# Recurrent mixer of a two-block network: scan exponentials issued as two steps, readouts one step behind the states, the output's square two steps ahead of its sum

## The reference, cut to what matters

```python
    def step(state, inp):
        qc, kc, gc, vc = inp
        L = jnp.cumsum(gc, axis=2)
        o_inter = jnp.einsum('bhtk,bhkv->bhtv', qc * jnp.exp(L), state)
        ...
        L_end = L[:, :, -1:, :]
        new_state = jnp.exp(L_end[:, :, 0, :])[..., None] * state + jnp.einsum(
            'bhsk,bhsv->bhkv', kc * jnp.exp(L_end - L), vc)
        return new_state, o_inter + o_intra
    ...
    o_fw, _ = hgrn2_chunk_scan(q, k_fw, g_fw, v, s_fw)
    o_bw, _ = hgrn2_chunk_scan(flip(q), flip(k_bw), flip(g_bw), flip(v), s_bw)
    return readout(o_fw + flip(o_bw), gate), y_c
```

## Time and profile before

| what | us |
|---|---|
| median of three runs | 3117.19 (3116.17 to 3118.52) |
| profiled execution | 3118.59 |
| its span | 3116.8 |
| TensorE busy | 2762.1 (89%) |
| VectorE busy | 1563.2 (50%) |
| ScalarE busy | 1029.5 (33%) |
| GpSimd busy | 1050.7 (34%) |
| mixer with dense products beside it, from 2180 to 2661 us | 481 |
| the last head alone, from 2661 to 2709 us | 48 |

### The profile page before, as it was taken

One profiled execution on the slowest core, in us unless ns is written; L12 is line 12 of the kernel. 1 busy time (PEld: TensorE's weight loads), 2 busy tenths in 40 slices (PEclk: granted clock), 3 DMA queues, 4 the chain that ended last, 5 costly groups with the idle time before them and its releaser, 6 DMA issues. The chain is left out here.

```text
span 3116.8 us, 37300 instructions
## 1 busy us (share of the span) xinstructions
PE 2762.1 (89%) x14376; PEld 2272.6 (73%) x14376; DVE 1563.2 (50%) x2423; ACT 1029.5 (33%) x1739; POOL 1050.7 (34%) x510
## 2 busy tenths in 40 slices
PE   1799869989999799999799999997888888699998
PEld 1587548868888577777588888875777777578886
DVE  3433435664454436565755555545556565532223
ACT  2323323232222434343421112124545444332222
POOL 2213343444444411110233223332434343334443
PEclk9899889999999899999899999998999999899999
DMA  5423222433333100000133333311111111022222
GB/s 194 147 88 107 90 83 100 154 122 135 128 129 129 64 18 24 18 23 20 49 127 116 121 115 122 129 62 39 55 41 48 41 48 41 28 81 95 95 95 75
DMA packets 78529, 264.56 MB, mean 85 GB/s; under 512 B 8464, under 2 KB 12688, under 8 KB 78352
## 3 DMA queue, kind: packets, MB, share of 16 engines
q1 hardware_dynamic: 70416, 248.67, 23.0%
q10 hardware_dynamic: 7648, 12.19, 1.2%
q0 software_dynamic: 288, 1.31, 0.1%
HBM read 258.99 MB, written 3.15 MB: 84 GB/s over the span
## 5 line engine op out<-in xcount | busy, mean ns | idle before, releaser
L1908 POOL TENSOR_TENSOR SLO<-RAW,SHI 128x1024 fp32r<-128x1024 f32 (+1 forms) x336 | 812.8, 2420 | 1691.3 <-ACT SHI L1753 1691.3
L1753 ACT ACTIVATE SHI<-RAW 128x1024 fp32r<-128x1024 f32 (+1 forms) x336 | 346.5, 1034 | 1183.9 <-PE PS L2165 1149.7
L2163 PE MATMUL PS<-HLh,SHI 128*128 128x512 f32 x1680 | 691.0, 411 | 21.4 <-DVE HLl L1973 14.3
L2164 PE MATMUL PS<-HLl,SHI 128*128 128x512 f32 x1680 | 662.6, 394 | 0.0
L2165 PE MATMUL PS<-HLh,SLO 128*128 128x512 f32 x1680 | 661.9, 394 | 0.0
L2163 PEld LDWEIGHTS PS<-HLh,SHI 128*128 128x128 f32 x1680 | 320.1, 191 | 115.6 <-issue 38.1
L2165 PEld LDWEIGHTS PS<-HLh,SLO 128*128 128x128 f32 x1680 | 319.7, 190 | 69.7
L2164 PEld LDWEIGHTS PS<-HLl,SHI 128*128 128x128 f32 x1680 | 320.8, 191 | 66.0 <-issue 8.1
L2163 PE MATMUL PS<-hh,SHI 128*128 128x512 f32 (+1 forms) x944 | 352.7, 374 | 11.4 <-DVE hl L2055 9.9
L2164 PE MATMUL PS<-hl,SHI 128*128 128x512 f32 (+1 forms) x944 | 348.4, 369 | 0.0
L2165 PE MATMUL PS<-hh,SLO 128*128 128x512 f32 (+1 forms) x944 | 348.0, 369 | 0.0
(11 more groups left out here) (229 smaller groups left out, 4048.3 us busy)
## 6 DMA issues: line engine op xcount, KB each, us to landing
RAW<-in_k_w SPq DMA_DIRECT2D x316, 512.0 KB, 3.2
ADA<-in_k_w SPq DMA_DIRECT2D x132, 512.0 KB, 4.1
early<-in_k_w SPq DMA_DIRECT2D x12, 512.0 KB, 10.8
RAW<-in_k_w SPq DMA_DIRECT2D x20, 256.0 KB, 2.6
XL<-in_xT ACTq DMA_DIRECT2D x1, 2048.0 KB, 12.0
bi<-in_k_bias ACTq DMA_DIRECT2D x16, 128.0 KB, 2.2
out<-XL SPq DMA_DIRECT2D x8, 256.0 KB, 2.1
bi<-in_k_bias ACTq DMA_DIRECT2D x8, 192.0 KB, 2.5
```

Of the source, the lines that this page charges most:

```text
L1753: eng.activation(u.hi, u.w, ACT.Copy).then_inc(S["a_hi"], 1)
L1908: eng.tensor_tensor(u.lo, u.w, u.hi.bitcast(F32), ALU.subtract).then_inc(S["g_lo"], 1)
L2163: eng.matmul(st.out, lh, rh, start=st.first and j == 0, stop=False)
L2164: eng.matmul(st.out, lh, rl, start=False, stop=False)
```

## The change

Three things change, all in the mixer.

1. `ScanE` becomes `ScanK` (keys) and `ScanQ` (queries). One generator now covers both directions. The keys' exponentials of d=1 are issued right after the transposes of d=0, and their transposes after the third readout of d=0. The queries' exponentials of d=1 are issued after the fourth readout of d=0, which they need because there is one `eq` buffer.
2. In a direction, state step n first makes its own matmul and then reads out the state of step n-1 (for n of 3 and 4, and the two last readouts follow in two further places).
3. `HOutA` loses its square, which becomes the step `HSquare`; two yields stand between the two.

```diff
-    def hscan(h, d, O, first):
+    def hscan(h, O):
...
+        def keys(d):
+            xcell, _, pend, _, t_pd = H[(h, d)]
+            ek = W["ek"].next()
+            t_eke[d] = tick("a_eke", 5 if d == 0 else 1)
+            put(ScanK(d, parts_of(xcell)[1], pend.ap, ek.ap, order[d], [xcell.rdy, t_pd], ek.free, t_eke[d]))
+            return ek
+
+        def queries(d):
...
+            put(ScanQ(d, parts_of(xcell)[0], pend.ap, eq.ap, q.ap, [xcell.rdy, t_pd], eq.free, q.rdy, t_eqe[d], t))
+            return eq, t
+
+        def turned(d, ek):
...
+                put(ScanT(ek.ap, kt.ap, order[d][n0:n1], n0, b.ap, t_eke[d], b.free, t, kt.free, t2))
...
+        def read(d, n, S, eq, t_eq):
...
+            put(ScanO(O.ap[:, 128 * j:128 * j + 128], S.ap, eq.ap[:, 128 * j:128 * j + 128], d == 0 and n == 0,
+                      [S.rdy, t_eq, O.free], t))
...
+        ek = keys(0)
         yield
...
+        eq, t_eq = queries(0)
         yield
...
+        kt, t_kt = turned(0, ek)
+        ek = keys(1)
+        yield
+        for d in range(2):
...
+                put(ScanS(b.ap[:, 0:128], kt.ap[:, 128 * n:128 * n + 128], vv[:, i, :], old.ap if S else None, S2.ap,
+                          dec.ap[:, i:i + 1], [t_kt[n], vc.rdy], b.free, t, [old.rdy if S else None, t_pd, S2.free], t2))
...
+                if n > 2:
+                    read(d, n - 3, S[n - 2], eq, t_eq)
+                yield
...
+            read(d, 2, S[3], eq, t_eq)
+            if d == 0:
+                kt, t_kt = turned(1, ek)
+            yield
+            t = read(d, 3, S[4], eq, t_eq)
+            eq.free = [t]
+            pend.free = [t_pd, t_eke[d], t_eqe[d]]
+            if d == 0:
+                eq, t_eq = queries(1)
+            yield
...
+            t1 = tick("a_osq")
+            put(HSquare(O.ap, f.ap, t, f.free, t1))
+            yield
+            yield
             b = take()
             work[0] += 2048
-            t1, t2, t3, t4 = tick("a_osq"), tick("p_ostat"), tick("a_oln"), tick("a_ors")
-            put(HOutA(O.ap, f.ap, b.ap, r.ap, t, f.free, t1, b.free, t2, r.free, t3, t4))
+            t2, t3, t4 = tick("p_ostat"), tick("a_oln"), tick("a_ors")
+            put(HOutA(f.ap, b.ap, r.ap, t1, b.free, t2, r.free, t3, t4))
```

More of the change, by code:

```diff
@@ L1480, in hscan @@
         vv = vc.ap.rearrange("p (t n) -> p t n", t=6)[:, :, 128 * (h % 2):128 * (h % 2) + 128]
[L1481 to L1488, removed]
@@ L1489, in hscan @@
-        yield
[L1490 to L1499, removed]
-        yield
[L1501 to L1504, removed]
-                work[0] += 512
[L1506 to L1520, removed]
-            yield
@@ L1522, in hscan @@
[L1522 to L1531, removed]
+        order = ([4, 5, 0, 1, 2], [5, 4, 3, 2, 1])
+        lats = ([0, 1, 2, 3], [3, 2, 1, 0])
+        t_eke, t_eqe = {}, {}
+        def keys(d):
[4 more added lines that the diff above has]
+            return ek
@@ new lines, in queries @@
+        def queries(d):
+            xcell, _, pend, _, t_pd = H[(h, d)]
+            eq = W["eq"].next()
+            t_eqe[d], t = tick("a_eqe", 1 if d == 0 else 4), tick("g_eqm")
+            put(ScanQ(d, parts_of(xcell)[0], pend.ap, eq.ap, q.ap, [xcell.rdy, t_pd], eq.free, q.rdy, t_eqe[d], t))
+            return eq, t
+        def turned(d, ek):
+            kt, t_kt = W["kt"].next(), []
+            for n0, n1 in ((0, 2), (2, 5)):
+                b = take()
+                work[0] += 512 * (n1 - n0)
+                t, t2 = tick("p_kt"), tick("a_kt")
+                put(ScanT(ek.ap, kt.ap, order[d][n0:n1], n0, b.ap, t_eke[d], b.free, t, kt.free, t2))
+                give(b, t2)
+                t_kt += [t2] * (n1 - n0)
+            ek.free = [t]
+            return kt, t_kt
@@ new lines, in read @@
+        def read(d, n, S, eq, t_eq):
+            j = lats[d][n]
+            work[0] += 512
+            t = tick("p_so")
+            put(ScanO(O.ap[:, 128 * j:128 * j + 128], S.ap, eq.ap[:, 128 * j:128 * j + 128], d == 0 and n == 0,
+                      [S.rdy, t_eq, O.free], t))
+            S.free.append(t)
+            return t
+        ek = keys(0)
+        yield
+        eq, t_eq = queries(0)
+        yield
+        kt, t_kt = turned(0, ek)
+        ek = keys(1)
+        yield
+        for d in range(2):
+            _, _, pend, dec, t_pd = H[(h, d)]
+            S = []
+            for n, i in enumerate(order[d]):
+                b = take()
+                work[0] += 512
+                S2, old = W["S"].next(), S[-1] if S else None
+                t, t2 = tick("p_sk"), tick("v_state")
+                put(ScanS(b.ap[:, 0:128], kt.ap[:, 128 * n:128 * n + 128], vv[:, i, :], old.ap if S else None, S2.ap,
+                          dec.ap[:, i:i + 1], [t_kt[n], vc.rdy], b.free, t, [old.rdy if S else None, t_pd, S2.free], t2))
+                S2.free, S2.rdy = [], [t2]
+                if S:
+                    old.free.append(t2)
+                give(b, t2)
+                S.append(S2)
+                if n > 2:
+                    read(d, n - 3, S[n - 2], eq, t_eq)
+                yield
+            kt.free = [t]
+            dec.free = [t2]
+            read(d, 2, S[3], eq, t_eq)
+            if d == 0:
+                kt, t_kt = turned(1, ek)
+            yield
+            t = read(d, 3, S[4], eq, t_eq)
[4 more added lines that the diff above has]
+            yield
@@ L1616, in hhead @@
         O = take()
-        sc = chain(hscan(h, 0, O, True), hscan(h, 1, O, False))
+        sc = hscan(h, O)
         alive = True
@@ L1942, in lev_a @@
                     eng.tensor_tensor(r, r, st.q, ALU.mult).then_inc(S["g_lev"], 1)
-            own = {Dma: dma_, Split: split, Square: square_, HRope: hrope, GateX: gate_x, DiagK: diag_k, ScanE: scan_e,
+            own = {Dma: dma_, Split: split, Square: square_, HRope: hrope, GateX: gate_x, DiagK: diag_k, ScanQ: scan_q,
                    LevA: lev_a}
```

39 lines of the change are left out of this document (22 added, 17 removed).

## The result

The changed kernel takes 3045.02 us (median of 4 runs, 3043.29 to 3048.43) against 3117.43 us for the kernel before beside it: a ratio of 0.9769, with a 95% interval of 0.9752 to 0.9786, or 72 us less. The forecast was 3054 us, 9 us too high and inside its range of 3036 to 3092. The profiled execution of the changed kernel took 3048.43 us (span 3046.6), so the two profiled executions are 70.2 us apart. One thing should be stated exactly, since the list of what changes says it otherwise (its second point): a readout now stands one state behind where it stood. It reads the state of step n-1 in the kernel before and the state of step n-2 now, next to the matmul of step n.

What follows compares the result with a forecast made beforehand. In the mixer TensorE has the most work yet idles, waiting in order for small results. Terms -14.4 - 10.6 - 7.5 - 22 - 2 - 13 + 12 - 7 = -64.5 from 3118.6 gave 3054 us, range 3036 to 3092.

Steps and rivals of the forecast that it cites:

- Backward keys: Backward transposes' 17.8 us of waits for the keys' exponentials go, 14.4 of them beside dense work: -14.4 us.
- Square and levels: Sum over the square stops waiting, -10.6 us; first-level product waits -12.3, new diagonal-product waits for key sum +4.8, together -7.5.
- Readouts: Readouts' waits for states outside the last head, 28.5 us, shrink to 6.5: -22 us, bounds 0 to -28.5.
- Forward keys: Of the forward transposes' 9.0 us of waits for the keys' exponentials, 2 us go; bounds 0 and -7.3.
- Clock: TensorE's slow spells behind nine waits of 2.7 us and more go, 1.5 us each: -13 us; bounds 0 and -14.
- What came back: A faster TensorE meets other results earlier, such as level products and `kt` copies: +12 us, between 0 and 23.
- the sign of being wrong that I had named for them: The forecast would be wrong if the copies of `kt` made the state matmuls wait; no size given.
- Last head: Last head alone: readouts off the update chain -3.2, backward keys 3, `HOutB` 1; -7 us, bounds -2 and -12.
- the one in which VectorE and ScalarE take the pace: A head's chain on VectorE and ScalarE sets the pace once the waits go: -34, 3084 us; chance 0.18.

Runs made afterwards that it cites:

- ke: Changed kernel with GpSimd's key sum issued earlier, ahead of the weight subtractions; 0.9736 of the kernel before, 10 us less than the changed kernel.
- f_k: Kernel before with only the keys' and queries' exponentials split and the backward keys issued earlier, readouts and square as before; ratio 0.9957 to it, -13 us.
- l2g: Changed kernel with the second level's product on GpSimd instead of VectorE; 0.9766 of the kernel before, no change against the changed kernel.

## Why the prediction was right, step by step

Taken by stage, the account holds. The profiled executions are 70.2 us apart. Beside dense work TensorE's idle time fell by 49.0 us, for which the terms of waits, with what I gave back, make 44.5; its busy time fell by 17.0 us, for which I had 13 of clock; the last head gave 4.7 where I had 7. Taken by part it holds less well, as follows.

*Backward keys (-14.4).* The waits went as said. The gain is 10 to 15 us by the four pairs of kernels that differ in this part alone (72 - 62, 57 - 46, 30 - 15, 13), and that includes the clock and the last head, for which I had 4.5 and 3 more. So this term was too large by a third or more. With the keys alone readouts wait longer, up to 5.21 us, behind a gate on VectorE; and with the readouts moved most of the keys' waits are gone without it.

*Square and levels (-10.6 and -7.5).* With three spells of clock and 1 us at the end my sum was -24; measured -15 to -17 in all four pairs. The square's 10.6 us and the first levels' 12.3 went: neither shows after, though 10.3 us at other levels do. The key sum's wait was foreseen as 2.4 us twice and is 2.26 and 2.27. Not foreseen was its 5.18 us in the last head, where it was 1.9. With the square alone, copies of `kt` cost 6.4 us, where the kernel before has 2.1.

*Readouts (-22).* This part was too small in the sum. With its clock and last head it made -30; measured are -42 to -47 us in the four pairs. Readouts waited 6.2 us in the end, where I had let 6.5 stay, so the term by itself is right; what the part takes along from the keys (14.4 us of waits beside dense work down to 4.9, by the place that it adds to a direction) and from the clock (11 us of busy time, 402.97 to 391.97) I had booked elsewhere or not at all.

*Forward keys (-2).* 9.0 became 6.8 us, but 3.07 of these are in the last head: beside dense work 7.3 became 3.7, so the term was too small by 1.6.

*Clock (-13).* TensorE's busy time beside dense work fell by 17.0 us between matching cuts, and the half-speed stretches, read in windows of 1 us, from ten to two. By the granted clock a stretch costs 1.7 us, where I had worked out 1.5 from 8 matmuls, so the eight that went make 13.7 of the 17.0 us; what the other 3.3 are was not found. I had counted nine, all behind waits of 2.7 us and more. The tenth stands behind a readout's wait of 2.05 us, and in the changed kernel both that stay follow a wait of 2.40 us, while a third such wait and the 3.10 us in the first head have none behind them. The length of the single wait, by which I had sorted them, does not decide.

*What came back (+12).* Level products now wait 10.3 us and the `kt` copies 3.3, 1.95 of these in the last head; before, the copies were waited for 2.1 us, so the sign of being wrong that I had named for them did not show in any size that counts. The size is right, the mechanism was open, and for the three waits of 2.40 us it is now known: a gate's wait on VectorE, not the exponentials' order on ScalarE.

*Last head (-7).* 42.3 against 47.0 us, -4.7. The key sum's wait grew from 1.9 to 5.18 us, behind the subtraction of 5.16. Here the parts do not add up: measured from the last dense matmul as for ke above, the last head is 4.9 us shorter with the keys alone, 4.7 with the readouts, 1.0 with the square and 4.9, not 10.6, with all three. With the key sum ahead of that subtraction (ke) it is 11.1 us shorter than before.

Booked by the part that brings it, the terms are keys -22, square -24, readouts -30, forward keys -2, and 12 given back; measured are 10 to 15, 15 to 17 and 42 to 47 us less, with nothing to give back in the sum. The mechanism was right, but that the forecast lies within 9 us of the result is partly luck: these errors go both ways. Of the rivals, the one in which VectorE and ScalarE take the pace is out as a price (3084 us), but its mechanism shows in three kernels, the changed one, f_k and l2g: VectorE waits in order for ScalarE, and small work that TensorE needs stands behind.

## What to carry to other kernels

When an engine with a full queue waits for small results of another, put more of its own work between the cause and the use (here the readout one state later, and with it one place more before the backward transposes); that part was worth 46 us where issuing the keys' exponentials earlier was worth 13, and it is the only one with which TensorE's clock came up. A list of waits books each delay on the first instruction that meets it: before you move the work of one wait, see what stands behind the same stall in the supplier's queue, for that will wait next (l2g: 2.40 us gone, 2.37 us come). Look at the orders of all queues at a boundary: a GpSimd sum of 1.3 us that stood one or two places too late cost some 10 us.

## What the hardware showed beyond that

- A GpSimd subtraction of 128x1024 takes 2.40 us; beside VectorE's differences it took 5.16 and in another kernel 5.21 us, more than twice as long. The Trainium skill (SBUF — State Buffer, Who interferes with whom) names this contention as one of a shared port pair; the trace agrees, and the size is larger here than the 1.30 against 2.01 us of the key sum. Which engine pays varies: at 2349.76 in the changed kernel the same subtraction took only 2.93 us beside VectorE's differences, and in the kernel before at 2374.86 it took 2.92 us while two passes of differences took 4.14 us, where another such pair took 1.28 (at 2667.41).
- Useless matmuls in waits made a kernel 7.5 us faster (4.1 to 10.9), through the clock; ones that overran the waits made it 4 us slower.
- Removing a wait of 2.7 to 3.5 us did not by itself bring clock back. With the keys or the square alone the granted clock fell to 0.94 and 0.95; with the readouts moved it rose to 0.98. Longer waits elsewhere (5.21 and 4.69 us for states) are a part of that, but not all: with the keys alone the three waits for the square are 3.54 us as before, and the clock lost 3.4 us at each, where it had lost 1.7. In that kernel it fell in the 2 us before such a wait ended; why was not found.
